# Hybrid decoder block on one core: the impulse response and the turning of the state-space tables move to later slots

## The reference, cut to what matters

```python
dt = jnp.exp(log_dt)[:, None]
mag = jnp.exp(lre * dt)
abar_re, abar_im = mag * jnp.cos(lim * dt), mag * jnp.sin(lim * dt)
bbar_re = f_re[..., None] * br - f_im[..., None] * bi
bu_re = jnp.einsum('blgh,gph->blgp', u32, bbar_re)
xr, xi = jax.vmap(scan_one)(bu_re, bu_im)          # x[t] = abar * x[t-1] + bu[t]
y = einsum(xr, c_re) - einsum(xi, c_im) + d * u32   # 48 groups of 16 channels, 64 states
```

## Time and profile before

| | |
|---|---|
| median of 3 runs | 2749.96 us (2745.32 to 2751.34) |
| profiled execution | 2747.44 us |
| its span, first to last instruction | 2745.6 us |
| granted TensorE clock, mean | 0.972 |
| PE busy | 2597.2 us, 95% of the span |
| DVE, ACT, POOL busy | 52%, 22%, 7% |

### The profile page before, as it was taken

One profiled execution on the slowest core, in us unless ns is written; L12 is line 12 of the kernel. 1 busy time (PEld: TensorE's weight loads), 2 busy tenths in 40 slices (PEclk: granted clock), 3 DMA queues, 4 the chain that ended last, 5 costly groups with the idle time before them and its releaser, 6 DMA issues. The chain is left out here.

```text
span 2745.6 us, 30607 instructions
## 1 busy us (share of the span) xinstructions
PE 2597.2 (95%) x12062; PEld 2084.2 (76%) x12062; DVE 1431.4 (52%) x2547; ACT 592.6 (22%) x1251; POOL 190.5 (7%) x330
## 2 busy tenths in 40 slices
PE   6899999999999999999999999999969699999997
PEld 4687777777778788887777778888857588888886
DVE  6427566765762333431444444344406477777785
ACT  4211112122121111111333334223214202020101
POOL 0000000000001111111000000011100000000000
PEclk9899999999999999999999999999989899999998
DMA  5122234233234555554133333467634475757571
GB/s 177 54 96 91 83 96 145 91 115 126 91 125 147 157 170 172 176 164 148 66 104 119 104 115 120 149 196 228 202 121 170 176 225 163 234 167 243 156 223 61
DMA packets 180947, 395.66 MB, mean 144 GB/s; under 512 B 26559, under 2 KB 68643, under 8 KB 174916
## 3 DMA queue, kind: packets, MB, share of 16 engines
q1 hardware_dynamic: 145652, 253.14, 30.2%
q0 software_dynamic: 35152, 140.55, 14.4%
HBM read 252.72 MB, written 140.88 MB: 143 GB/s over the span
## 5 line engine op out<-in xcount | busy, mean ns | idle before, releaser
L136 PE MATMUL bank<-h_hi,w_hi 128*128 128x512 f32 (+1 forms) x2208 | 912.9, 413 | 19.2 <-DVE w_lo L130 16.5
L138 PE MATMUL bank<-h_hi,w_lo 128*128 128x512 f32 (+1 forms) x2208 | 874.8, 396 | 0.0
L137 PE MATMUL bank<-h_lo,w_hi 128*128 128x512 f32 (+1 forms) x2208 | 874.4, 396 | 0.0
L136 PEld LDWEIGHTS bank<-h_hi,w_hi 128*128 128x128 f32 x2208 | 422.2, 191 | 130.8 <-issue 24.3
L138 PEld LDWEIGHTS bank<-h_hi,w_lo 128*128 128x128 f32 x2208 | 420.5, 190 | 97.5
L137 PEld LDWEIGHTS bank<-h_lo,w_hi 128*128 128x128 f32 x2208 | 422.2, 191 | 92.2 <-issue 1.7
L128 DVE CAST w_hi<-w_raw 128x1024 fp32r<-128x1024 f32 (+1 forms) x130 | 89.4, 687 | 397.0 <-PE bank L138 318.4
L770 ACT ACTIVATE ev<-bank 128x512 f32<-128x512 f32 x112 | 66.6, 597 | 505.4 <-PE bank L138 497.5
L130 DVE TENSOR_TENSOR w_lo<-w_raw,w_hi 128x1024 fp32r<-128x1024 f32 (+1 forms) x130 | 157.7, 1213 | 4.5
L635 POOL DMA_DIRECT2D proj_d<-ev x160 | 87.8, 549 | 987.5 <-ACT ev L768 608.1
L1171 DVE COPY ptr<-bank 128x512 f32<-128x512 f32 x80 | 51.5, 686 | 187.6 <-PE bank L1444 187.6
(11 more groups left out here) (242 smaller groups left out, 3409.7 us busy)
## 6 DMA issues: line engine op xcount, KB each, us to landing
proj_d<-ev POOLq DMA_DIRECT2D x160, 256.0 KB, 3.3
w_raw<-w_in SPq DMA_DIRECT2D x68, 512.0 KB, 4.9
gt<-proj_d POOLq DMA_DIRECT2D x32, 768.0 KB, 7.8
proj_d<-ev POOLq DMA_DIRECT2D x22, 1024.0 KB, 4.2
w_raw<-w_br SPq DMA_DIRECT2D x32, 512.0 KB, 4.3
space<-w_br SPq DMA_DIRECT2D x32, 512.0 KB, 4.8
mats<-mats_d SPq DMA_DIRECT2D x48, 320.0 KB
space<-o_d SPq DMA_DIRECT2D x14, 1024.0 KB, 7.2
```

Of the source, the lines that this page charges most:

```text
L136: nc.tensor.matmul(out, ah, bh, start=(start and n == 0), stop=False)
L137: nc.tensor.matmul(out, ah, bl, start=False, stop=False)
L138: last = nc.tensor.matmul(out, al, bh, start=False, stop=(stop and n == len(pairs) - 1))
```

## The change

The impulse response on PE goes from slot 2 to slot 4, the transposes from slot 4 to slot 6. On DVE `response` goes from slot 4 to the head of slot 5, and `turned_inputs` from slot 6 to slot 7. On SP `keep_response` goes from slot 5 to slot 6. No instruction is added or removed.

```diff
--- before.py   (SP)
+++ after.py
                             if w == 4:
                                 keep_states(u)
-                            if w == 5:
+                            if w == 6:
                                 keep_response(u)
-                            if w == 6:
                                 keep_cosines(u, 0)
...               (DVE)
-                            elif w == 4:
+                            elif w == 5:
                                 response(u)
-                            elif w == 5:
                                 cosines(u, 0)
                                 angles(u, 1)
-                            elif w == 6:
+                            elif w == 7:
                                 turned_inputs(u)
...               (PE)
-                        if w == 2:
+                        if w == 4:
                             pe.wait_ge(ca_ready, u + 1)
...
-                        if w == 4:
+                        if w == 6:
                             pe.wait_ge(ba_ready, u + 1)
```

## The result

The changed kernel takes 2684.11 us, the median of 4 runs (2683.89 to 2685.24), beside 2747.64 us for the kernel before in 4 runs (2743.02 to 2751.34). The ratio is 0.977, with a 95% interval of 0.9757 to 0.9782: 63.5 us less. The forecast was 2680 us in a range of 2672 to 2702.

A forecast was written before the change was run, and what follows sets the result against it. The prediction took PE, busy for 95% of the span, to bound the kernel. The profiled 2747.4 us less 69.1 us gave 2678.3 us; from the median of 2749.96 us, 2680.9 us. Forecast 2680 us, range 2672 to 2702 us.

The forecast's parts named there:

- Where PE loses time now: PE waits 44.0 us for DVE's `ca` at the impulse response, in 12 waits; low clock behind takes another 23 us.
- the wait is paid twice: At the impulse response PE stands still, then its matmuls run slowly at 1.2 GHz: 46 us plus 23 us.
- The price: In the table stage, moving the impulse response from slot 2 to 4 gives back 69.1 us over 12 units.
- base of 12.35 us: PE's interval from last matmul before the group to the transposes, without pause at full clock: 0.23 + 0.97 + 48 x 0.2323.
- 0.97 us for the group: The impulse response's four matmuls at full clock, taken from unit 1; uncertainty over 12 units -0.7 to +3 us.
- The moves at no cost: Response on DVE, transposes and `turned_inputs`, stores on SP and copies on ACT: each claimed to cost 0.
- ACT's copies: Slot 6's chunk copied by about 347.9, before PE needs the bank for next unit's slot 1: 6.5 us to spare.
- The clock falling without a pause: Rival: the narrow group and short stops around it lower PE's clock anyway, so only 46 us return: 2701 us, chance 0.08.
- A part of the wait staying in the units with values: Rival: units 2 to 4 give nothing, so 25.6 us are missing: 2704 us, chance 0.05.
- The gain lost again later: Rival: after the tables, the first load or the `ys_lo` wait eats the gain: 2747 us, chance 0.03.
- Slower by ACT's chain: Rival: ACT's wait for the cosines' store holds slot 6's chunk copy beyond PE's slot 1: 2780 us, chance 0.02.

The follow-up runs named there:

- the kernel with `ca` first: The kernel before, slots as they were, but DVE makes `ca` before `cas`, so `ca` is ready earlier: 2704.21 us, ratio 0.9847.

## Why the prediction was right

*Where PE loses time now.* Right. The wait for `ca` went from 44.0 us to none, and the clock that fell behind it came back: in the table stage it is 1.00 throughout. That the wait is paid twice is shown by the kernel with `ca` first, where 28.4 us less wait gave 41.3 us, and by the units whose clock no longer falls there.

*The price.* 69.1 us was worked out, 63.5 and 64.6 us were measured. That the time missed by less, 2684.11 against 2680.9 us, was luck: the median it was taken from, 2749.96 us of 3 runs, was 2.3 us above the 2747.64 us of the 4 runs, and this made up for part of it. The stage after the tables begins at 789.3 us instead of 855.5: 66.2 us were gained where the change acts. The sum's base of 12.35 us for an interval was too short by 0.25 us: without a pause it is 12.60 us (605.10 to 617.70 in unit 8). Most of this is 0.33 us from the last matmul before the group to its start where I took 0.23, and 0.34 us instead of 0.23 behind it. In 12 units this is 3 us, the whole gap between 69.1 and 66.2 us within the stage. The term that the prediction called least sure, 0.97 us for the group, was exact. The rest, 1.6 to 2.7 us, lies in stretches that the change doesn't touch and that vary as much from run to run.

*The moves at no cost.* Right for all of them: the response on DVE, the transposes and their copies, and SP's stores brought no new wait of PE. The slacks came out near what was reckoned: in unit 2 the last instruction of `ca` ends at 312.57 and PE comes at 318.52, 5.95 us later (5.9 reckoned), and in unit 8 the group is over at 606.48 and DVE reads it at 607.88, 1.4 us later (1.3 reckoned). For ACT's copies the prediction had the wrong first reader where values are turned: the turning in slot 0, with 5.8 us, and not the bank in slot 1, with 6.6 (6.5 reckoned). It cost nothing here, and two slots more use either up. Nor was ACT nearest to PE by the prediction's own numbers, which gave `ca` 5.9 us.

*The rivals.* The clock falling without a pause: refuted by the profile after and by the group at full speed behind 0.49 and 1.29 us. This was the rule of the page "TensorE: Matmul & The Clock Gate" of the Trainium skill, section "A second HAM failure mode: psum-queue depth-cycling"; here matmuls that change between three banks kept a granted clock of 1.00 over 579.6 us, and stops of 0.49 and 1.29 us did not swing it. A part of the wait staying in the units with values: no such wait. The gain lost again later: the stages behind are as long as before, within 3 us. Slower by ACT's chain: this mechanism is real, but even with the response four slots later than it was it costs 31 to 34 us (2715.19 against the changed kernel's 2684.11 and 2681.51), not the 69 that it would have to.

## What to carry to other kernels

A wait of the busiest engine costs more than its idle time if its clock falls behind it. Count the interval from a matmul well before to one well behind, not the pause; in this kernel it was half as much again. When side work is put into fixed slots between large matmuls, look for the slot in which its input is ready with a small reserve: one slot later gave everything here, two gave nothing more, and four broke another chain. If a table moves two jobs at once, undo each alone, for one of them may carry all.

## What was unexpected of the hardware

How long PE may pause before its clock falls to 1.2 GHz is not a sharp length. It never fell behind pauses of 0.49 and 1.29 us, fell in four of nine units behind 2.0 to 2.1 us, in all nine units of the kernel before behind 2.8 to 2.9 us, and behind every pause of 3.7 to 6.1 us. Why it fell in every second unit behind the same 2.07 to 2.09 us, no run here shows. After 2.08 us in three of the four, and once after 2.88, the fall came about 1 us or more into the work that followed, so the group that had waited ran at full speed and others paid. What a fall costs beyond the pause is not fixed either. In unit 7 of the kernel before it cost 17.05 - 12.60 - 2.95 = 1.5 us, where 2.95 is what the pause adds to the 0.33 us ahead of a group; this is as much as behind 2.08 us. In unit 0, behind a pause of the same kind (2.83 us), it cost 18.23 - 12.60 - 2.90 = 2.7 us, for the clock stayed low about twice as long: its mean is 0.55 over 6.8 us, while in unit 7 it is 0.54 over 3.7 us and 1.00 behind them. PE's windows in unit 0 and unit 7, the clock again third from the end:

```profile
212.70:219.50 6.80, 6.78 (x21) 0.55 0.28 77
...
594.30:598.00 3.70, 3.69 (x13) 0.54 0.51 142
598.00:608.00 10.00, 10.00 (x45) 1.00 0.27 108
```
